# A decoder layer on one core: weight splits of dense items behind the turned weights' residue, head copies behind the tanh, and attention steps spread over more items

## What is computed

```python
u = rmsnorm(x) @ w_in                          # xl, gl | q, k, v
lru_out = gated_linear_recurrence(conv(xl)) * gelu(gl)
w = softmax(q1 @ k1.T * s + mask) - lam * softmax(q2 @ k2.T * s + mask)     # 4 heads
att_out = rmsnorm(w @ v, subln_g) * (1 - lam_init)
x = x + rmsnorm(concat(lru_out, att_out) @ w_out)
f = (silu(h @ w_gate) * (h @ w_up)) @ w_down   # h = rmsnorm(x), d_ff 2816
x = x + rmsnorm(f)
x = x + rmsnorm(sigmoid(x @ ple_w_gate) * (p @ ple_w_proj))
```

## Time and profile before

| | us |
|---|---|
| median of 3 runs (3135.62 to 3139.99) | 3136.3 |
| the profiled execution, its own time | 3138.19 |
| span of the profiled execution, first to last instruction | 3136.4 |
| PE busy within the span | 2962.7 |
| DVE, ACT, POOL busy | 1779.9, 1376.4, 218.9 |
| mean granted clock of PE, as a share of 2.4 GHz | 0.972 |

### The profile page before, as it was taken

How to read it: one execution, slowest core, us unless ns; L and a number is a source line. 1 busy time by engine, 2 the same in 40 slices (tenths; PEclk the granted TensorE clock), 3 DMA queues, 4 the chain that set the end, 5 groups by cost and what they waited for, 6 DMA issues and landing times.

```text
span 3136.4 us, 38465 instructions
## 1 busy us (share of the span) xinstructions
PE 2962.7 (94%) x14384; PEld 2409.6 (77%) x14384; DVE 1779.9 (57%) x2858; ACT 1376.4 (44%) x2501; POOL 218.9 (7%) x314
## 2 busy tenths in 40 slices
PE   7999999779999999999999999999999999999997
PEld 6778787657677777877787778777888777787875
DVE  6767746467336666565465555655666555334454
ACT  5654625444234445454444444544444444222233
POOL 0201100200000100001111000001010000000000
PEclk9999989879999999999999999999999999999998
DMA  5536432846653443553443335534432344232221
GB/s 177 191 128 232 132 125 78 251 141 212 184 146 106 121 118 112 172 144 107 132 118 88 103 109 168 155 91 128 111 106 76 110 149 136 85 99 81 84 74 55
DMA packets 377576, 402.59 MB, mean 128 GB/s; under 512 B 25641, under 2 KB 277845, under 8 KB 377392
## 3 DMA queue, kind: packets, MB, share of 16 engines
q1 hardware_dynamic: 360624, 341.32, 36.9%
q0 software_dynamic: 16768, 58.81, 5.2%
HBM read 341.19 MB, written 58.91 MB: 128 GB/s over the span
## 4 chain that ended last, share of the span: by engine, by line
PE 61%; DVE 12%; ACT 3%; issue 2%; DMA 0%; SPq 0%; DVEq 0%; POOL 0%; ACTq 0%; POOLq 0%
PE c_bank L2610 49%; PE b_S L2902 3%; PE b_WT L2914 2%; DVE c_w L2290 2%; PE b_O L2928 2%; DVE b_m L2490 1%; PE b_S L2619 1%; PE b_O L2619 1%; ACT c_junk L2062 1%; DVE c_rows L2301 1%; DVE c_rows L2308 1%; PE b_S L2882 1%; PE b_O L2930 1%; DVE b_p L2497 1%; DVE c_act L2402 1%
## 5 line engine op out<-in xcount | busy, mean ns | idle before, releaser
L2610 PE MATMUL c_bank<-c_hT,c_w 128*128 128x512 f32 (+1 forms) x4416 | 1041.1, 390 | 15.4 <-DVE c_hT L2328 15.4
L2610 PEld LDWEIGHTS c_bank<-c_hT,c_w 128*128 128x128 f32 x4416 | 804.8, 192 | 173.6 <-issue 18.2
L2290 DVE TENSOR_TENSOR c_w<-c_raw,c_w 128x1024 fp32r<-128x1024 f32 x334 | 405.4, 1220 | 196.9 <-ACT c_w L2041 195.6
L2610 PE MATMUL c_bank<-c_w,c_fT 128*128 128x512 f32 x2112 | 506.7, 393 | 0.0
L2041 ACT ACTIVATE c_w<-c_raw 128x1024 fp32r<-128x1024 f32 x334 | 351.1, 1054 | 286.7 <-PE c_bank L2610 246.4
L2610 PEld LDWEIGHTS c_bank<-c_w,c_fT 128*128 128x128 f32 x2112 | 391.7, 188 | 87.3 <-issue 3.4
L2219 ACT ACTIVATE b_p<-b_S,b_nm 128x512 f32<-128x512 f32 (+3 forms) x288 | 180.2, 631 | 522.8 <-DVE b_nm L2491 522.8
L898 PE MATMUL a_bank<-a_w,a_hT 128*128 128x512 f32 (+1 forms) x1224 | 300.5, 401 | 0.0
L2610 PE MATMUL c_bank<-c_w,c_hT 128*128 128x512 f32 x1152 | 270.4, 393 | 7.3 <-DVEq L2373 3.7
L898 PEld LDWEIGHTS a_bank<-a_w,a_hT 128*128 128x128 f32 (+1 forms) x1224 | 220.8, 183 | 61.4 <-issue 3.8
L2610 PEld LDWEIGHTS c_bank<-c_w,c_hT 128*128 128x128 f32 x1152 | 218.1, 190 | 54.4 <-issue 4.1
(11 more groups left out here) (363 smaller groups left out, 3354.4 us busy)
## 6 DMA issues: line engine op xcount, KB each, us to landing
c_raw<-in_ffn_w_gate SPq DMA_DIRECT2D x88, 512.0 KB, 5.0
c_raw<-in_ffn_w_up SPq DMA_DIRECT2D x88, 512.0 KB, 4.2
c_raw<-in_ffn_w_down SPq DMA_DIRECT2D x88, 512.0 KB, 4.0
a_raw<-in_w_in SPq DMA_DIRECT2D x40, 1024.0 KB, 5.2
b_k<-split_kT SPq DMA_DIRECT2D x72, 256.0 KB, 4.9
b_v<-split_v SPq DMA_DIRECT2D x36, 512.0 KB, 3.6
c_raw<-in_w_out SPq DMA_DIRECT2D x32, 512.0 KB, 5.0
c_raw<-in_ple_w_gate SPq DMA_DIRECT2D x32, 512.0 KB, 4.2
```

Of the source, the lines that this page charges most:

```text
L2290: V.tensor_tensor(w[:, e[1] % SLOTS, 1], raw[:, n % RAW], w[:, e[1] % SLOTS, 0].bitcast(F32), ALU.subtract).then_inc(split_ready, 1)
L2610: ins = T.matmul(out, lhs(k, a), rhs(k, b), start=first and k == 0 and n == 0, stop=end and k == blocks - 1 and n == 2)
```

## The change

Three edits, all in `feed`. Nothing is added or removed: the instructions of each engine and their sizes stay, only the order and the places change.

1. **Places.** The `down 2 0` items of all three groups and the `pg 0` items become places; the special case for group 0 goes. 153 places become 171, and the 150 ticks are spread over them: about every eighth place carries none, where before three places in all did.
2. **Splits late.** At `gate`, `up` and `down` items that both score and value, `split_first` moves on ACT behind the copy of the turned weights (L2228), and `split_second` on DVE behind their residue (L2509). Items of other kinds (`pg` among them), and items that only score or only value, split where they did.
3. **Head copy.** ACT's copy `oT` of a finished head moves behind the tanh.

```diff
-    PLACES = [n for n, (i, item) in enumerate(ALL) if i < LAST and item[0] in ("gate", "up", "down") and item[:2] != ("down", 2)]
+    PLACES = [n for n, (i, item) in enumerate(ALL) if i < LAST and (item[0] in ("gate", "up", "down") or item[:2] == ("pg", 0))]
...
-    PLACES = sorted([n for n in PLACES if n > FINISH + 3] + [at[0, ("down", 2, 0, kp)] for kp in range(3)])
+    PLACES = [n for n in PLACES if n > FINISH + 3]
...
+    def split_late(n):
+
+        return ALL[n][1][0] in ("gate", "up", "down") and scored(n) is not None and valued(n) is not None
...
-                x = finished(n, 2)
-                if x is not None and x % 4 == 3:
-                    act.wait_ge(o_turned, x // 4 + 1)
-                    wait_if_any(act, stored, 16 * (x // 4))
-                    A.activation(oT[:], WT[:], ACT.Copy, scale=sub_gain[:]).then_inc(out_ready, 1)
...
                         A.activation(s_f[:], s_gu[:, 0], ACT.Tanh, scale=0.5).then_inc(sg_silu, 1)
+                x = finished(n, 2)
+                if x is not None and x % 4 == 3:
+                    act.wait_ge(o_turned, x // 4 + 1)
+                    wait_if_any(act, stored, 16 * (x // 4))
+                    A.activation(oT[:], WT[:], ACT.Copy, scale=sub_gain[:]).then_inc(out_ready, 1)
...
-                for e in SPLITS[n][item == ("proj", 0):]:
-                    split_first(e)
+                if not split_late(n):
+                    for e in SPLITS[n][item == ("proj", 0):]:
+                        split_first(e)
...
                     A.activation(wT[:, 0, 0:size(s)], WT[:, 0:size(s)], ACT.Copy).then_inc(wt_hi, 1)
+                if split_late(n):
+                    for e in SPLITS[n]:
+                        split_first(e)
                 if was[0] in ("up", "far"):
...
-                for e in SPLITS[n][item == ("proj", 0):]:
-                    split_second(e)
+                if not split_late(n):
+                    for e in SPLITS[n][item == ("proj", 0):]:
+                        split_second(e)
...
                     V.tensor_tensor(wT[:, 1, 0:size(s)], WT[:, 0:size(s)], wT[:, 0, 0:size(s)].bitcast(F32), ALU.subtract).then_inc(wt_lo, 1)
+                if split_late(n):
+                    for e in SPLITS[n]:
+                        split_second(e)
                 if was[0] in ("up", "far"):
```

## The result

The changed kernel takes 3147.5 us (median; 3142.56 to 3151.16), the kernel before, run beside it on the same chip, 3139.0 (3135.62 to 3143.95): a ratio of 1.0025, with an interval of 1.0014 to 1.0037. The forecast was 3123 and its range ended at 3142. The profiled execution after took 3142.6 us, 4.4 more than the one before.

A forecast was written before the change was run, and what follows sets the result against it. PE bound the kernel, busy 2962.7 of 3138.2 us, some 80 us winnable; 26 + 19.6 - 25 - 9 - 9 + 10 = 13 us won gave 3123 us, range 3104 to 3142.

The forecast's parts named there:

- signs of being wrong: No PE wait at L2928; mean clock under 0.97 between 914 and 2450; DVE waits for ACT's split much over 0.3 us.
- Part 6: PE's low clock in attention: three falls in eight head waits, 5 us instead of 15, so 10 us won.
- Rival 1: PE's clock falls at eight head waits and eight 1.2 us waits, from short-wait series: 41 us, 3159 us; chance 0.1.
- Parts 1 and 2: PE's waits for `b_p`: late split wins 26 us after `up` items, head copy and places 19.6 us at five heads.
- part 3: At tile ends, DVE empties `b_O` behind the late split, so PE waits 0.55 to 1.2 us at 34 tiles: 25 lost.
- part 5: New places in `pg 0` and at the `downt 0` bank: waits of 1.1 to 2.4 us, 9 us lost.
- Part 4: After a head's fourth tile, sums, root and normalisation end 1.5 us later at eight heads: 9 us lost (-5 to 20).
- rival 2: DVE has no slack ahead of the tanh products: the late split wins 13 us less, 3136 us; chance 0.2.
- rival 3: PE comes to `b_O` later than thought, so the new wait doesn't show at tile ends or heads: 3092 us, chance 0.1.
- rival 4: Table switches drain: the head chain is longer by 1.38 us at eight heads, 11 in all: 3134 us, chance 0.05.

The follow-up runs named there:

- the version with the output first: The changed kernel with the late split behind the tile's output where a tile ended one tick ago: 3102.0 us, ratio 0.9874.
- the third experiment: The changed kernel with a head's transposes, copy and store one tick later: 3136.4 us, ratio 0.999.

## Why the prediction was wrong, point by point

The mechanisms were named right, each wait stood where it was said to stand, and the sum still came out on the wrong side: 13 us won was forecast, and the items lost 6.6 (the spans of the two profiled executions differ by 4.4). The sum was a small rest of large terms, 56 to be won against 43 to be lost, so a few us in each were enough. Its signs of being wrong did not show it: the wait for `b_O` is there, the mean clock between 914 and 2450 was 0.99, and DVE waits for ACT's half of a late split 0.3 us as a rule. They ask whether the mechanisms are there, and not on which side the sum comes out. The terms, as forecast and as the table above and the version with the output first give them:

| part | forecast | measured |
|---|---|---|
| 1 and 2, waits for `b_p` that go | +45.6 | about +38.5 |
| 3, the wait for `b_O` | -25 | -28.7 |
| 4, the head's chain | -9 | -7.8 |
| 5, new places | -9 | about -10 |
| 6, the clock | +10 | +1.6 |

**Part 6, the clock, was the step that failed worst.** I took three falls in eight head waits, since waits up to 1.65 us had rarely drawn one in the earlier trace rows and 3.67 had. Six of the eight drew one, one of them twice as long. In the items with attention the clock stood at 1.2 GHz for 27.3 us after and 30.7 before, which costs 13.7 and 15.3. The forecast had 5. The error was to price each wait alone: ahead of a head PE waits for `b_O` and, after eight products, again for the head (1.08 and 1.78 in the rows above), and the falls come with this pair. In the three versions that have it (after the change, with the old places, and without edit 3) 21 of 25 such heads have a fall. Without the first of the two (output first, on either list of places, where the second is 1.1 to 1.6) none of 18 heads has one, and none without the second (the head one tick later). It is not only that the second wait is shorter there: of eight waits of 1.8 to 2.0 for `b_p`, in three versions, one has a fall. How close the two waits must stand is open: with 1.0 or 1.1 for `b_p` and 1.6 for the head half an item later (the early split at tiles' ends) none of four heads has a fall. Rival 1 named the right cause and asked for too much of it: sixteen falls where there were seven. Its other half, falls from the series of short waits, is refuted by the third experiment. The Trainium skill, TensorE: Matmul & The Clock Gate, section A second HAM failure mode: psum-queue depth-cycling, expects frequent short idles of PE between groups of matmuls to let the clock swing; it gives no length for them, and 43 waits of at most 1.1 us in that run did not.

**Parts 1 and 2** were right in kind: no wait of 3.7 is left, and edit 3 alone is worth 8.8, most of it by the clock. The heads' items gave 24.4 instead of 19.6; before the change they also held five of the 32 short waits, 5.6 us, so the two parts cannot be told apart. The short waits gave less than the 26: besides the rests of 0.2 to 0.4 that the forecast named, three tile ends behind the four additions of a `down` part keep 1.2 to 1.7 us each, because there 2.5 us of additions stand ahead of the maxima. With the output first these items cost 4.2 us in all, nearly the whole rest of 4.5 that I had allowed. The 38.5 is 24.4 from the heads' items, 5.5 from those behind an `up`, 6.1 from the tiles' ends (16.3 to 10.2, the last from the version without part 3), 0.3 from other items, and 2.2 that the bank of `downt` takes from these kinds (L2358 in the list of waits) and that is part 5's. It is "about", since the items' roles differ between before and after.

**Part 3** had its count to the item (34 tiles: 22 ordinary, eight behind an `up`, four behind the additions) and its mechanism, and a price a little low: 0.73 us for an ordinary tile's end and 1.3 behind an `up`, where 0.55 and 1.2 were said. The missing 0.18 shows in the rows of `up 5`: PE's first product into `b_O` starts 2.52 us behind the start of DVE's residue (1436.34 to 1438.86), and 1.86 with the output first (1427.62 to 1429.48). So it comes 0.66 later, and that product then takes 0.36 us instead of 0.28.

**Part 4** is the best of the sum. The items before a head were to take 2.7 us more, and 3.3 behind an `up`: they take 2.70 and 3.30 or 3.31 (10.5 and 11.1 in the table of stretches). Against 16.3 before, 24.1 after is 7.8 lost.

**Part 5**: `pg 0 0` cost 1.60, 1.61 and 1.13 where 1.65, 1.65 and 1.15 were said; `pg 0 2` of group 0 took 2.95 and a fall of 1.7 instead of 2.4 (two splits ahead of the maxima, a wait of 2.45, the clock at 0.86 in the row above).

**Rivals 2, 3 and 4** did not come. The waits of DVE ahead of the tanh products left items behind an `up` at 4.7 us for 42 items (rival 2 asked for 13 more than forecast); the wait for `b_O` shows in the list (rival 3; its price of 31 us should have been 34 by the forecast's own terms, 25 and 9); and the activation behind the root's table load starts 0.01 us after it, 1562.59 + 1.28 against 1563.88, as in the earlier trace rows (rival 4).

**The range** ended at 3142 because the bad ends of parts 3, 4 and 6 had been left to rival 1 as one case. Three of five terms erring by 4 to 8 us in the same direction was the likelier way to the slow side, and had no chance of its own. Put together, the errors are 7.1 in parts 1 and 2, then 3.7, -1.2, 1 and 8.4: 19.0 us, of the 19.6 between +13 and -6.6. The rest up to 3147.5 is the spread between executions: the profiled one after was the fastest of its six, at a mean granted clock of 0.976, and the other five stood at 0.974 or 0.975. By an estimate from these means (0.001 of some 3145 us is 3 us) they lost 3 to 6 us more to the clock; in which part of the execution is not known, but the 1.6 of part 6 is likely on the good side.

What the forecast did have in hand and did not use is the remedy. Part 3 says that the output "stands behind the split now", and that is no property of a late split. One place further back it costs nothing, 45 us are won, and the heads' waits and falls shrink with it.

## What to carry to other kernels

When work is moved to the back of an in-order queue, look for the last instruction there that another engine needs within the same pass, here the one that frees a PSUM bank, and put the moved work behind that one; a place that is late for one consumer is early for the next. When a forecast is a small rest of large terms, price the waits that go and those that come by one measure (here the length of the item: a shown wait of 0.51 cost 0.73), and price waits of the same engine that follow each other closely as one when the clock is at stake. A wait that is removed by moving a step one pass on should be followed to what queues behind the step that stayed: the third experiment lost a good part of its gain to a table load that had been hidden under the wait.

## What the runs showed of the chip that was not expected

The clock's falls go with the length and the pairing of waits and not with their number. At heads where a wait of 1.8 followed one of 0.5 to 1.1, 21 of 25 have a fall (six of eight after the change, seven of nine with the old places, eight of eight without edit 3). At heads with one wait of 1.1 to 1.6 and the output first none of 18 has; the kernel before has one, at 1.63. Beside 43 waits of at most 1.1 us and no wait for a head there is none at a head. At waits for `b_p`, over the eleven profiled executions, the falls are: one at eight of 1.8 to 2.0, one at three of 2.1, six at nine of 2.44 to 2.61, one at two of 3.0 to 3.1, and six at six of 3.66 to 3.77. So the same wait draws a fall in one execution and none in the next (`pg 0 2` of group 0, 2.45 us, has one after the change and none without edit 3), and a forecast can give a fall a chance, not a place.

The part of the execution that none of the versions touches is not constant. PE began the item `gate 9` of group 0 between 912.3 and 923.0 us in the eleven profiled executions, with falls of the clock in different places ahead of it. A pair of spans can therefore differ by 10 us for no reason in the change; the output-first version's span shows 37.7 us won over the changed kernel where its items show 48.7 and the medians 45.5.
